# The 256-column low products of a unit, set one by one between the 512-column high products of the next unit

## The chip, the cores and the metric

One core of a Trainium2 chip runs the whole program. The metric is the device time of one execution in microseconds, the median of three runs. Nothing is read from other cores.

## The reference

Two transformer blocks of two layers each work on 256 tokens of width 1024. Around the change only the gated feed-forward layers matter. There are six of them: two in each of the two layers of the first block, and one in each of the two layers of the second. With h the normed and modulated input, each computes

```python
def swiglu(h, w_gu, w_down):
    g, u = jnp.split(h @ w_gu, 2, axis=-1)
    return (jax.nn.silu(g) * u) @ w_down
```

with w_gu of 1024 x 5632 and w_down of 2816 x 1024, in float32. The second block writes the same thing out in line. Between the feed-forward layers stand attention and retention stages, which the change leaves alone.

## The kernel before, in words

**High and low parts.** A float32 matmul is made of products in fp32r. Each operand is split into a high part (the rounded value) and a low part (the rest), and three products are added up in PSUM: high by high, low of the activations by high of the weights, and high of the activations by low of the weights. ScalarE makes the high part of a weight unit (hi_static, L810), VectorE the low part (lo_static, L1355).

**Units and the ring.** Weights come in units of 128 x 1024 float32 (512 KB). SyncE loads them in pairs into a ring of six raw slots; high and low parts have a ring of seven slots each (PARTS). ScalarE may write slot n only when unit n - 7 is used up, which TensorE tells by adding one to mm_done behind the last product of every unit; VectorE takes unit n after hi_done has counted it, and SyncE refills a raw slot after lo_done.

**A feed-forward phase.** The 2816 hidden columns are worked on in 11 strips of 256. Of a strip b, four units hold gate and up weights and two hold the down weights of the strip before. In strips from FIRST_TURNED on (from strip 3 in the first phase, from strip 1 in the five others, 58 strips in all) the weights are the stationary operand: turned_unit (L2363) works on one half strip j (128 hidden columns) and one half q of the contraction. It issues eight *high* products, whose moving operand is 512 columns (high and low part of the 256 tokens side by side, tile hT), with weights_hi stationary (L2368), and then, after waiting for lo_done, eight *low* products of 256 columns (the tokens' high part) with weights_lo stationary (L2373). Units of a strip come in the order (j=0,q=0), (0,1), (1,0), (1,1). The sums of half strip j lie in the two PSUM banks half_banks(j): columns 0 to 255 hold high by high, columns 256 to 511 hold the two cross terms.

**Behind the half strip.** When mm_done has counted the second unit of a half strip, ScalarE copies the cross part (cross, L1004), VectorE adds it (half_sum, L1690), ScalarE applies silu (L1009), VectorE multiplies gate and up (L1695), ScalarE makes the high part of the activation (L1014, ahi) and VectorE the low part (L1703, alo). Between these steps both engines convert weight units in a fixed written order, and VectorE also works off modulation units (mod_unit, L1368), up to six a strip. TensorE may start half strip j of strip b + 1 when half_sum of strip b, half j, is done.

**Down.** After the four turned units of strip b, down (L2377) multiplies the activations of strip b - 1 by its two down units: rows_unit (L2161) issues for each unit eight products of 512 columns with ahi and alo stationary and weights_hi moving (L2169), and after lo_done four with weights_lo moving (L2174), all into banks 0 to 3. In the last strip of a phase only one down unit is done so; last_three (L2178) takes the other three, and waits there for ahi_done and alo_done of the last strip.

The order of the work on every engine is written out by hand; nothing is planned by a program. The statements at the core:

```python
for kind in (1, 0):
    for k in range(4):
        T.matmul(half_banks(j)[:, kind, :], whi[...], hx[:, :, 4 * q + k, :], ...)
pe.wait_ge(S("lo_done"), n + 1)
for kind in (1, 0):
    for k in range(4):
        ins = T.matmul(half_banks(j)[:, kind, 256:512], wlo[...], hhi[:, 4 * q + k, :], ...)
ins.then_inc(S("mm_done"), 1)
```

Of the kernel before, what the change touches and what calls it, by code (L numbers as in the profile page):

```python
# [261 lines left out]
def build(nc, A, out):  # L262
    with ExitStack() as ctx:
# [1867 lines left out]
        def _(pe):  # L2131
# [29 lines left out]
            def rows_unit(slot, ready, c, first, last, hi_, lo_, first_bank=0, act=None):  # L2161

                pe.wait_ge(S("hi_done"), ready)
                for i, src in enumerate((hi_, lo_)):
                    if act is not None:
                        pe.wait_ge(S(("ahi_done", "alo_done")[i]), act)
                    for t in range(NT):
                        for h in range(2):
                            T.matmul(bank[first_bank + 2 * t + h][:, :], src[:, c, P * t:P * (t + 1)], whi[:, slot, 512 * h:512 * (h + 1)],  # L2169
                                     start=first and i == 0, stop=False)  # L2170
                pe.wait_ge(S("lo_done"), ready)
# [161 lines left out]
            for kind, n0, a in phases:  # L2333
# [19 lines left out]
                if kind == "ffn":  # L2353
# [9 lines left out]
                    def turned_unit(n, j, q):  # L2363

                        pe.wait_ge(S("hi_done"), n + 1)
                        for kind in (1, 0):
                            for k in range(4):
                                T.matmul(half_banks(j)[:, kind, :], whi[:, n % PARTS, 256 * k + P * kind:256 * k + P * (kind + 1)], hx[:, :, 4 * q + k, :],  # L2368
                                         start=q == 0 and k == 0, stop=False)
                        pe.wait_ge(S("lo_done"), n + 1)  # L2370
                        for kind in (1, 0):
                            for k in range(4):
                                ins = T.matmul(half_banks(j)[:, kind, 256:512], wlo[:, n % PARTS, 256 * k + P * kind:256 * k + P * (kind + 1)], hhi[:, 4 * q + k, :],  # L2373
                                               start=False, stop=q == 1 and k == 3)
                        ins.then_inc(S("mm_done"), 1)

                    def down(c, j, u0=0, u1=2):  # L2377
                        if FIRST_TURNED[f] == 1 and j == 0:
                            pe.wait_ge(S("alo_done"), STRIPS * f + 1)
                        for u in range(u0, u1):  # L2380
                            rows_unit((c + u) % PARTS, c + u + 1, u, j == 0 and u == 0, False, ahi[:, j % 2], alo[:, j % 2], act=STRIPS * f + j + 1)
# [27 lines left out]
                    for b in range(FIRST_TURNED[f], STRIPS):  # L2409
                        c = n0 + 4 + 6 * (b - 1)  # L2410
                        for j in range(2):
# [8 lines left out]
                            turned_unit(c + 2 * j, j, 0)  # L2420
# [5 lines left out]
                            turned_unit(c + 2 * j + 1, j, 1)  # L2426
                            if b == 1 and j == 0:
                                turn(0, 0)
                        if b < STRIPS - 1:
                            down(c + 4, b - 1)  # L2430
# [476 lines left out]
```

## Time and profile before

| | |
|---|---|
| Median of 3 runs | 1761.82 us (1761.37 to 1762.06) |
| Span of the profiled execution, first to last instruction | 1759.8 us |
| Its own time as a run | not listed; the span is 2.0 us under the median of the runs |
| TensorE (PE) busy | 1732.4 us, 98% of the span |
| TensorE weight loads (PEld) busy | 1470.0 us, 84% |
| VectorE (DVE) busy | 1419.2 us, 81% |
| ScalarE (ACT) busy | 1006.7 us, 57% |
| Granted TensorE clock, mean | 0.999 of full |
| Chain that ended last | TensorE 94%, of it L2368 24% and L2373 12% |

The profile is one execution. "Busy" of TensorE is the union of its matmul records; since matmuls are pipelined, a record is longer than the distance to the next one's start (a 512-column product has a record of 389 ns, and the next starts 227 ns after it). What a product costs the engine is therefore read from the distances between starts, or from the chain of waits, whose pieces are laid end to end.

### The profile page before, as it was taken

The page shows a single profiled execution, that of the slowest core. Times are in us where ns is not written, and L with a number is a line of the kernel's source. Part 1 is how long each engine was busy: PE and PEld are TensorE (multiplying, and loading weights), DVE is VectorE, ACT ScalarE, POOL GpSimd, SP SyncE. Part 2 cuts the span into 40 slices and gives each one's busy share as a digit, 9 for nine tenths or more (in the row PEclk, how much of TensorE's full clock was granted, in tenths as well). Part 3 has the DMA queues.
Part 4 walks back from the last instruction along what each step waited for, and adds up shares of the span by engine and source line. Part 5 has one row for each costly group of instructions (what it writes and reads, how often), then busy time and mean ns, then how long its engine had stood idle before and what let it go on. Part 6 is the DMA issues. An engine that isn't in the chain of part 4 may idle for free.

```text
span 1759.8 us, 24720 instructions
## 1 busy us (share of the span) xinstructions
PE 1732.4 (98%) x9178; PEld 1470.0 (84%) x9178; DVE 1419.2 (81%) x2185; ACT 1006.7 (57%) x1666; POOL 184.0 (10%) x382
## 2 busy tenths in 40 slices
PE   6999999999999999999999999999999999999998
PEld 3888888888888888988888888888888888888886
DVE  7899987898899888878888866579888876688565
ACT  5445577755475556877545644556455544465454
POOL 3021012111111111021110000001110000010000
PEclk9999999999999999999999999999999999999999
DMA  9999742699869985418898654459886483466551
GB/s 352 356 360 393 273 147 83 259 332 337 315 225 340 332 314 205 168 51 317 329 334 291 224 206 158 161 191 333 324 325 249 169 301 146 185 229 245 204 194 70
DMA packets 125144, 441.10 MB, mean 251 GB/s; under 512 B 15248, under 2 KB 18272, under 8 KB 124896
## 3 DMA queue, kind: packets, MB, share of 16 engines
q1 hardware_dynamic: 91024, 316.17, 49.1%
q0 software_dynamic: 33296, 120.12, 18.2%
q10 hardware_dynamic: 704, 3.23, 0.5%
q8 instruction: 73, 1.20, 0.3%
q14 instruction: 47, 0.39, 0.1%
HBM read 438.38 MB, written 1.09 MB: 250 GB/s over the span
## 4 chain that ended last, share of the span: by engine, by line
PE 94%; DVE 2%; DMA 2%; ACT 1%; issue 1%; SPq 0%; DVEq 0%; ACTq 0%
PE banks L2368 24%; PE banks L2169 15%; PE banks L2373 12%; PE banks L2147 11%; PE banks L2174 7%; PE banks L2152 6%; PE banks L2317 2%; PE banks L2321 2%; PE banks L2326 2%; PE banks L2137 1%; PE banks L2139 1%; PE banks L2138 1%; DMA weights_raw<-in_w_mod_first 1%; PE banks L2281 1%; DVE weights_lo L1355 1%
## 5 line engine op out<-in xcount | busy, mean ns | idle before, releaser
L1355 DVE TENSOR_TENSOR weights_lo<-weights_raw,weights_hi 128x1024 fp32r<-128x1024 f32 (+2 forms) x584 | 685.9, 1200 | 67.5 <-ACT weights_hi L810 66.7
L810 ACT ACTIVATE weights_hi<-weights_raw 128x1024 fp32r<-128x1024 f32 (+2 forms) x584 | 584.8, 1036 | 68.3 <-PE banks L2174 21.9
L2368 PE MATMUL banks<-hT,weights_hi 128*128 128x512 f32 x1856 | 464.1, 392 | 0.0
L2368 PEld LDWEIGHTS banks<-hT,weights_hi 128*128 128x128 f32 x1856 | 337.3, 189 | 63.0
L2373 PEld LDWEIGHTS banks<-hT,weights_lo 128*128 128x128 f32 x1856 | 253.2, 190 | 18.1
L1368 DVE CUSTOM_DVE_ANT_0 arena<-arena,mod_acc,vectors 128x1024 f32<-128x1024 f32 x216 | 267.6, 1280 | 0.0
L2373 PE MATMUL banks<-hT,weights_lo 128*128 128x256 f32 x1856 | 258.8, 282 | 0.0
L1004 ACT ACTIVATE arena<-banks 128x512 f32<-128x512 f32 x116 | 69.3, 598 | 323.1 <-PE banks L2373 322.9
L2147 PE MATMUL banks<-weights_hi,hT 128*128 128x512 f32 (+2 forms) x896 | 218.2, 385 | 0.0
L2147 PEld LDWEIGHTS banks<-weights_hi,hT 128*128 128x128 f32 x896 | 165.6, 188 | 29.9
L1690 DVE TENSOR_TENSOR arena<-banks,arena 128x512 f32<-128x512 f32 x116 | 79.8, 688 | 108.9 <-ACT arena L1004 108.9
L2169 PE MATMUL banks<-weights_hi,actT_hi 128*128 128x512 f32 x520 | 140.9, 392 | 0.3 <-DVE window_bias L1405 0.3
L2169 PE MATMUL banks<-weights_hi,actT_lo 128*128 128x512 f32 x520 | 139.3, 390 | 0.0
L2174 PE MATMUL banks<-weights_lo,actT_hi 128*128 128x512 f32 x520 | 139.0, 389 | 0.0
L2152 PE MATMUL banks<-weights_lo,hT 128*128 128x512 f32 (+2 forms) x448 | 116.9, 383 | 0.0
L2169 PEld LDWEIGHTS banks<-weights_hi,actT_lo 128*128 128x128 f32 x520 | 97.6, 188 | 21.1
L2174 PEld LDWEIGHTS banks<-weights_lo,actT_hi 128*128 128x128 f32 x520 | 97.6, 188 | 20.3
L2169 PEld LDWEIGHTS banks<-weights_hi,actT_hi 128*128 128x128 f32 x520 | 93.6, 189 | 16.8 <-DVE window_bias L1405 0.7
L531 POOL DMA_DIRECT2D arena<-in_w_mod x128 | 67.5, 530 | 364.8 <-DVE mod_cols L1368 361.2
L2152 PEld LDWEIGHTS banks<-weights_lo,hT 128*128 128x128 f32 x448 | 83.8, 188 | 15.1
L1009 ACT ACTIVATE arena<-arena 128x256 f32<-128x256 f32 x116 | 48.0, 414 | 74.1 <-DVE arena L1690 74.0
L792 POOL TENSOR_TENSOR x<-x,arena 128x512 f32<-128x512 f32 x10 | 12.7, 1275 | 677.1 <-DVE arena L1513 677.1
(358 smaller groups left out, 1971.3 us busy)
## 6 DMA issues: line engine op xcount, KB each, us to landing
weights_raw<-in_w_ffn_gu SPq DMA_DIRECT2D x176, 512.0 KB, 4.5
arena<-in_w_mod POOLq DMA_DIRECT2D x128, 512.0 KB, 6.2
weights_raw<-in_w_in SPq DMA_DIRECT2D x104, 512.0 KB, 4.1
weights_raw<-in_w_ffn_down SPq DMA_DIRECT2D x88, 512.0 KB, 5.0
arena<-in_w_ada POOLq DMA_DIRECT2D x88, 512.0 KB, 5.6
weights_raw<-in_w_ffn_in SPq DMA_DIRECT2D x88, 512.0 KB, 4.1
weights_raw<-in_w_ffn_out SPq DMA_DIRECT2D x44, 512.0 KB, 4.5
weights_raw<-in_w_out SPq DMA_DIRECT2D x32, 512.0 KB, 3.8
```

The lines of the kernel that those rows point to most:

```text
L531: eng.dma_start(mod_tile(m), mod_rows(m)).then_inc(S(mod_sem(m)), 16)
L810: nc.scalar.activation(whi[:, n % PARTS, 0:width], raw[:, slot, 0:width], ACT.Copy).then_inc(S("hi_done"), credit(n))
L1004: nc.scalar.activation(cross_t[:, j], half_banks(j)[:, :, 256:512], ACT.Copy).then_inc(S("half_by_act"), 1)
L1355: V.tensor_tensor(wlo[:, n % PARTS, 0:width], raw[:, n % RING, 0:width], whi[:, n % PARTS, 0:width].bitcast(F32), ALU.subtract).then_inc(S ...
L1368: V.tensor_tensor_reduce(modw[m % MOD_RING], modw[m % MOD_RING], cond_row, 1.0, vec[:, m:m + 1], ALU.mult, ALU.add, modc[:, m:m + 1])\
L1690: V.tensor_tensor(sum_t[:, j], half_banks(j)[:, :, 0:256], cross_t[:, j], ALU.add).then_inc(S("half_by_dve"), 1)
L2147: T.matmul(bank[banks[t]][:, 0:width], src[:, 2 * u + k, P * t:P * (t + 1)], whi[:, slot, k * width:(k + 1) * width], start=u == 0 and k = ...
L2152: ins = T.matmul(bank[banks[t]][:, 0:width], hi_[:, 2 * u + k, P * t:P * (t + 1)], wlo[:, slot, k * width:(k + 1) * width], start=False, s ...
L2169: T.matmul(bank[first_bank + 2 * t + h][:, :], src[:, c, P * t:P * (t + 1)], whi[:, slot, 512 * h:512 * (h + 1)], start=first and i == 0, ...
L2174: ins = T.matmul(bank[first_bank + 2 * t + h][:, :], hi_[:, c, P * t:P * (t + 1)], wlo[:, slot, 512 * h:512 * (h + 1)], start=False, stop= ...
L2368: T.matmul(half_banks(j)[:, kind, :], whi[:, n % PARTS, 256 * k + P * kind:256 * k + P * (kind + 1)], hx[:, :, 4 * q + k, :], start=q == 0 ...
L2373: ins = T.matmul(half_banks(j)[:, kind, 256:512], wlo[:, n % PARTS, 256 * k + P * kind:256 * k + P * (kind + 1)], hhi[:, 4 * q + k, :], st ...
```

## The change

Three things are new.

1. turned_unit gets the unit before it (before). If there is one, it waits for that unit's lo_done at its own start, and behind each of its eight high products it issues one low product of the unit before (turned_low). The eighth adds to mm_done for the unit before.
2. The low products of the strip's fourth unit go into the first down unit: rows_unit issues one behind each of its eight products with weights_hi moving.
3. In the last strip of a phase the fourth unit's low products stand in a block behind it (last_low), as before. The first unit of a strip has no low products between its high ones.

The products, their operands, the PSUM regions and the number of instructions on ScalarE, VectorE, GpSimd and SyncE are the same.

```diff
-            def rows_unit(slot, ready, c, first, last, hi_, lo_, first_bank=0, act=None):
+            def rows_unit(slot, ready, c, first, last, hi_, lo_, first_bank=0, act=None, low=None, turned_low=None):
...
                             T.matmul(bank[first_bank + 2 * t + h][:, :], src[:, c, P * t:P * (t + 1)], whi[:, slot, 512 * h:512 * (h + 1)],
                                      start=first and i == 0, stop=False)
+                            if low is not None:
+                                turned_low(low, 4 * i + 2 * t + h)
...
-                    def turned_unit(n, j, q):
+                    def turned_low(unit, i):
+
+                        n, j, q = unit
+                        kind, k = 1 - i // 4, i % 4
+                        ins = T.matmul(half_banks(j)[:, kind, 256:512], wlo[:, n % PARTS, 256 * k + P * kind:256 * k + P * (kind + 1)], hhi[:, 4 * q + k, :],
+                                       start=False, stop=q == 1 and k == 3)
+                        if i == 7:
+                            ins.then_inc(S("mm_done"), 1)
+
+                    def turned_unit(n, j, q, before):
 
                         pe.wait_ge(S("hi_done"), n + 1)
...
+                        if before is not None:
+                            pe.wait_ge(S("lo_done"), before[0] + 1)
+                        for i in range(8):
+                            kind, k = 1 - i // 4, i % 4
+                            T.matmul(half_banks(j)[:, kind, :], whi[:, n % PARTS, 256 * k + P * kind:256 * k + P * (kind + 1)], hx[:, :, 4 * q + k, :],
+                                     start=q == 0 and k == 0, stop=False)
+                            if before is not None:
+                                turned_low(before, i)
+
+                    def last_low(unit):
+
+                        pe.wait_ge(S("lo_done"), unit[0] + 1)
+                        for i in range(8):
+                            turned_low(unit, i)
+
+                    def down(c, j, u0=0, u1=2, low=None):
                         if FIRST_TURNED[f] == 1 and j == 0:
                             pe.wait_ge(S("alo_done"), STRIPS * f + 1)
+                        if low is not None:
+                            pe.wait_ge(S("lo_done"), low[0] + 1)
                         for u in range(u0, u1):
-                            rows_unit((c + u) % PARTS, c + u + 1, u, j == 0 and u == 0, False, ahi[:, j % 2], alo[:, j % 2], act=STRIPS * f + j + 1)
+                            rows_unit((c + u) % PARTS, c + u + 1, u, j == 0 and u == 0, False, ahi[:, j % 2], alo[:, j % 2], act=STRIPS * f + j + 1,
+                                      low=low if u == 0 else None, turned_low=turned_low)
...
-                            turned_unit(c + 2 * j, j, 0)
+                            turned_unit(c + 2 * j, j, 0, (c + 1, 0, 1) if j == 1 else None)
...
-                            turned_unit(c + 2 * j + 1, j, 1)
+                            turned_unit(c + 2 * j + 1, j, 1, (c + 2 * j, j, 0))
+                            if b == STRIPS - 1 and j == 1:
+                                last_low((c + 3, 1, 1))
...
-                            down(c + 4, b - 1)
+                            down(c + 4, b - 1, low=(c + 3, 1, 1))
```

## Rows read from the trace of the kernel before

**Rows 1.** The page, part 1: busy us, share of the span, instructions of each engine.

```profile
PE 1732.4 (98%) x9178; PEld 1470.0 (84%) x9178; DVE 1419.2 (81%) x2185; ACT 1006.7 (57%) x1666; POOL 184.0 (10%) x382
```

**Rows 2.** The page, part 5: groups of the two kinds of product, and ScalarE's wait.

```profile
L2368 PE MATMUL banks<-hT,weights_hi 128*128 128x512 f32 x1856 | 464.1, 392 | 0.0
...
L2373 PE MATMUL banks<-hT,weights_lo 128*128 128x256 f32 x1856 | 258.8, 282 | 0.0
L1004 ACT ACTIVATE arena<-banks 128x512 f32<-128x512 f32 x116 | 69.3, 598 | 323.1 <-PE banks L2373 322.9
```

**Rows 3.** Chain of waits, 592 to 625 us, one strip: start us, us, what.

```profile
592.39 1.81 PE banks L2368 x8
594.20 0.95 PE banks L2373 x8
595.16 1.84 PE banks L2368 x8
597.00 0.95 PE banks L2373 x8
597.95 1.84 PE banks L2368 x8
...
602.58 0.95 PE banks L2373 x8
603.54 1.84 PE banks L2169 x8
605.38 0.91 PE banks L2174 x4
```

**Rows 4.** Chain of waits, 240 to 258 us: products of other widths.

```profile
247.44 1.29 PE banks L2147 x8
248.73 0.54 PE banks L2152 x4
...
250.87 0.17 PE banks L2137
251.04 0.17 PE banks L2138
...
253.78 0.76 PE banks L2152 x4
```

**Rows 5.** Timeline of TensorE, same place: widths of those products (start us, us).

```profile
248.57 0.70 PE L2152 MATMUL banks<-weights_lo,actT_hi 128*128 128x288 f32 x4
...
250.71 0.33 PE L2137 MATMUL banks<-weights_hi,actT_hi 128*128 128x384 f32 x1
...
253.61 0.92 PE L2152 MATMUL banks<-weights_lo,hT 128*128 128x416 f32 x4
```

**Rows 6.** Timeline of TensorE, 610 to 613.6 us, in windows that begin ever later.

```profile
610.65 1.11 PE L2373 MATMUL banks<-hT,weights_lo 128*128 128x256 f32 x8
611.61 0.63 PE L2368 MATMUL banks<-hT,weights_hi 128*128 128x512 f32 x2
...
610.77 1.00 PE L2373 MATMUL banks<-hT,weights_lo 128*128 128x256 f32 x7
...
611.84 1.77 PE L2368 MATMUL banks<-hT,weights_hi 128*128 128x512 f32 x7
...
612.08 1.53 PE L2368 MATMUL banks<-hT,weights_hi 128*128 128x512 f32 x6
```

**Rows 7.** Busy time in two strips: us, PE, PEld, DVE, ACT, POOL, clock, DMA.

```profile
114.61:131.23 16.62, 16.62 (x90) 14.34 (x88) 16.62 (x25) 8.46 (x12) 3.75 (x8) 1.00 0.96 361
608.84:625.45 16.61, 16.61 (x89) 14.34 (x88) 14.41 (x21) 8.45 (x13) 2.11 (x4) 1.00 0.90 329
```

**Rows 8.** Timeline, 126 to 137 us: half_sum and TensorE's next use of its banks.

```profile
131.13 0.69 DVE L1690 TENSOR_TENSOR arena<-banks,arena 128x512 f32<-128x512 f32 x1
...
136.79 0.40 PE L2368 MATMUL banks<-hT,weights_hi 128*128 128x512 f32 x1
```

**Rows 9.** Timeline, 495 to 506 us: last strip of the second feed-forward phase.

```profile
495.65 2.00 PE L2368 MATMUL banks<-hT,weights_hi 128*128 128x512 f32 x8
...
495.85 0.60 ACT L1004 ACTIVATE arena<-banks 128x512 f32<-128x512 f32 x1 [5.16 <-PE banks L2373]
...
499.38 1.99 ACT L810 ACTIVATE weights_hi<-weights_raw 128x1024 fp32r<-128x1024 f32 x2
...
501.44 0.60 ACT L1004 ACTIVATE arena<-banks 128x512 f32<-128x512 f32 x1
...
503.71 0.42 ACT L1014 ACTIVATE actT_hi<-arena 128x256 fp32r<-128x256 f32 x1 [0.49 <-DVE arena L1695]
...
505.35 0.39 PE L2196 MATMUL banks<-weights_hi,actT_hi 128*128 128x512 f32 x1
```

More of the change, by code:

```diff
@@ L2361, in _ @@
                     rows_made = made_by_rows(f)
-                    def turned_unit(n, j, q):
-                        pe.wait_ge(S("hi_done"), n + 1)
[L2366 to L2375, printed above, removed]
@@ L2377, in down @@
-                    def down(c, j, u0=0, u1=2):
+                    def turned_low(unit, i):
[5 more added lines that the diff above has]
+                            ins.then_inc(S("mm_done"), 1)
```

## Prediction

> **What bounds the kernel now.** I read the shares first: TensorE is busy 98% of the span [rows 1]. Then the costliest groups: the 1856 high products and the 1856 low products of the turned strips, neither with idle time before it [rows 2]. In the 58 turned strips TensorE never waits, so only the distance from one product to the next can give time, or a new wait can take some. The chain of waits shows these distances without the pipeline's overlap [rows 3]. The reader should see three sizes there. Eight high products behind products of 512 columns take 1.81 us, 226.7 ns each. Eight high products behind a low block take 1.84 us, whether they are turned or down products. Eight low products take 0.95 us, 119 ns each. The granted clock is full in these strips [rows 7].
>
> **What a product costs.** Can the order matter at all? The other widths answer [rows 4, 5]. Four products of 288 columns take 0.54 us (about 133 ns each), one of 384 columns 0.17 us once the stretch has settled, one of 512 columns 226.7 ns, one of 256 columns inside a block about 120 ns. From 256 to 288, 384 and 512 columns the cost grows by about 0.417 ns a column, which is the full clock of 2.4 GHz, and what is left over is the same everywhere: 226.7 - 213.3 = 13.3 ns, and 120 - 106.7 = 13.3 ns. One width is off: 416 columns take 190 ns, 3 more than this line gives. So a low product in its block is not held up by something the wide ones hide; it pays the same fixed 13.3 ns (an estimate, read from these widths). A high and a low product side by side then cost 226.7 + 120.0 = 346.7 ns in any order.
>
> What order can change is the rest. From the second low of a block (610.77) to the first high (611.61) seven lows take 0.84 us, 120 ns each [rows 6]. The whole block takes 0.953 us, so its first low is followed after 113 ns. The highs behind it take 1.841 us instead of 1.813: the first three start at 611.61, 611.84 and 612.08 [rows 6], 0.47 us for two distances that would be 0.453. Low block and highs behind it cost 2.794 us, 349.2 ns for a high and a low, and the 2.5 ns over 346.7 are a tax that the first five or so highs pay. (Check on a strip: 24 x 0.2267 + 4 x 2.794 = 16.62 us; it takes 16.61 [rows 7].)
>
> **The change, part by part.** *Moved:* 58 strips have 4 low blocks each, 232. Six of them (the last unit of each phase) stay in a block with a down unit behind them, and cost what they did. The other 226 are taken apart and go among the 226 blocks of eight highs behind them, 174 turned ones and 52 of the down units. Before: 226 x (0.953 + 1.841) = 631.4 us. After: 1808 pairs at p ns each.
>
> *The bounds of p*, which no row shows, since nowhere before do 512 and 256 columns alternate. From below: the first low product behind a high one is followed after 113.3 ns (as above), and the high before it costs 226.7. If each low behaved as the first of a block and each high as behind a high, p = 340.0, the sum 614.7 us, 16.7 us less. From above: lows at 120 and each high with the mean tax of the highs behind a block, 27.6 / 5 = 5.5 ns (1.841 - 1.813 = 0.028 us over the five that pay it), p = 352.2, the sum 636.8, 5.4 us more. In between lie the fixed cost alone, p = 346.7 (626.8, 4.6 us less), and the same tax per low product as now, p = 349.2 (no change). I take 348.0, the middle of the last two: 629.2 us, **2.2 us less**. Nearest to the pair by its mean of 384 columns is the stretch of 384 columns, whose late products take 0.17 us [rows 4], that is 2 x 173.3 = 346.7 a pair; some of its early ones take 0.18, so part of the tax may stay. That the short first distance counts in full I do not believe, because the first high behind a block gives the 6.7 ns back (0.23 in place of 0.227, the two first ones 0.47 in place of 0.453): the two look like one shift of the start.
>
> The Trainium skill ("TensorE: Matmul & The Clock Gate", on weight loading and the back-to-back gap) says that TensorE pulls weight loads ahead of running matmuls, and puts a load of 128 columns at P/1.2, an estimate of 107 ns here; by it a load fits behind either kind of product. It also states a fixed cost of 2.5 ns a product at full clock, which would make a pair 325 ns; the distances of 226.7 and 120 ns in rows 3 disagree, and they decide.
>
> *The waits of TensorE.* Each paired unit now waits for hi_done and for the earlier unit's lo_done at its start. The first is satisfied long before: ScalarE and VectorE are a strip's part ahead, and no idle time stands before L2368 or L2373 [rows 2]. The second is the wait that stood ahead of the low block, now asked for at the same point of the work. A unit that already waits for two semaphores (597.95, the half strip j = 1) takes the same 1.84 us as one that waits for one (595.16) [rows 3], so one wait more is costed at nothing. Its cover is the running product; without it, each would be some tens of ns.
>
> *mm_done comes later.* A unit's last low product now ends behind the next unit's eight pairs: 8 x 0.227 = 1.8 us later. Who waits for it: ScalarE's copy L1004 (it waits 322.9 us in all for L2373, 105 times [rows 2]), behind it in ScalarE's order the next weights' high parts, behind these VectorE's low parts and SyncE's refills. ScalarE has some 8 us idle in a strip of 16.6 [rows 7], so it catches up. The tightest place in mid-phase is the first phase, where VectorE has no idle time at all in a strip [rows 7]: half_sum ends at 131.82 and TensorE wants the banks at 136.79 [rows 8], 5.0 us of room against 1.8. VectorE there is set by its modulation units, not by the copy. Costed at nothing; if the room went, each strip would lose what is missing.
>
> *The ends of the phases.* The copy for j = 0 of the last strip would start at about 497.6 instead of 495.85 [rows 9]. ScalarE then works without a break through two single conversions, silu, the high part and a double conversion that now ends at 501.37 and would end near 502.7. The copy for j = 1, ready since 501.4, goes from 501.44 to about 502.7, and the activation's high part, which ends at 504.13, to 505.4. TensorE asks for it at 505.35 [rows 9]. So the next thing late is ahi_done, by 0.05 to 0.3 us, in five phases (in the first, VectorE's modulation units set the chain already): **0.7 us more** in all, between 0 and 1.5.
>
> Sum against the profiled execution: 1759.8 - 2.2 + 0.7 = 1758.3 us of span; the median of the runs is 2.0 us above the span, so 1761.8 - 1.5 = **1760.3 us**.
>
> **The rivals.** What a measurement of this kernel can tell from no change is about 0.2%, 3.5 us.
>
> *A. The low product is held up in its block by the weight load beside it* and is free between wide ones: p = 340, 1761.8 - 16.7 + 0.7 = 1745.8 us. For it speaks the first distance of each block, 113 ns; against it that 288 and 384 columns, which leave a load more time, have the same 13.3 ns over their columns. Chance 0.12.
>
> *B. Each high behind a low pays the tax.* Now five of eight highs behind a low block pay, in alternation all eight would be just behind a low one. Price 5.5 ns a pair over 346.7, 1808 times: 1761.8 + 5.4 + 0.7 = 1767.9 us, slower. It decides from p = 350.8 on (3.5 us less the 0.7, over 1808 pairs). For it: the first two highs behind a block pay some 16 ns together, more than half of the 28, and products of 416 columns keep 3 ns too many through a whole stretch [rows 4]. Against: if the tax is a backlog of narrow products that wide ones work off, one low leaves an eighth of it. Chance 0.18.
>
> *C. Nothing, to the last ns:* p = 349.2 and the phase ends hidden, 1761.8. It is within the likeliest case.
>
> *D. The delayed mm_done reaches TensorE in every strip.* 1.8 us against 5.0 us of room makes it unlikely; 58 strips x 0.3 us would be 17 us. Chance 0.02.
>
> **How the numbers follow.** Likeliest, 0.68: p between 346.7 and 349.2 with 0 to 1.5 us at the phase ends, 1757.2 to 1763.3 us. A 0.12, B 0.18, D 0.02. Most of the likeliest case lies within 0.2%; its low edge, p at 346.7, does not, and gets 0.15 of the chance. So faster 0.12 + 0.15 = 0.27, slower 0.18 + 0.02 = 0.20, same 0.53. The range takes in the bounds of p at both ends, since nothing in the trace excludes either: 1745 to 1768.5.
>
> **What would show it.** In the chain of waits of the changed kernel a strip's first unit should still be eight highs in 1.81 us; eight pairs behind it 2.77 to 2.79 us (2.72 if A holds, 2.82 if B), and a whole strip 16.57 us against 16.61 now. L1004 should wait for a product under another line, its cross copies in mid-phase 1.8 us later against the strip, without idle time of TensorE. At the phase ends a gap of up to 0.3 us should stand before L2196. The forecast is wrong if single distances behind a low product are longer than 127 ns or behind a high one longer than 232, if TensorE's idle time in the turned strips is no longer nil, or if pairs run at 340.

## The result, and the profile after

The changed kernel takes **1777.18 us** (median of 4 runs, 1776.62 to 1778.14), the kernel before, run beside it, 1761.94 us (4 runs, 1761.37 to 1762.61). The ratio is 1.0086, 95% interval 1.0072 to 1.0100: slower by 15.2 us. The forecast was 1760.3 with a range up to 1768.5; it is wrong in size and in sign. The profiled execution has a span of 1774.8 us (its own time 1776.62) at a granted clock of 0.998.

The page of the changed kernel: the busy time of each engine, and the groups that answer to [rows 1, 2] (busy us, mean ns of one, idle time before them and what ended it).

```profile
PE 1741.5 (98%) x9178; PEld 1466.7 (83%) x9178; DVE 1420.3 (80%) x2185; ACT 1004.6 (57%) x1666; POOL 184.0 (10%) x382
...
L2381 PE MATMUL banks<-hT,weights_hi 128*128 128x512 f32 x1856 | 599.1, 396 | 0.0
L2369 PE MATMUL banks<-hT,weights_lo 128*128 128x256 f32 x1856 | 512.4, 280 | 0.0
...
L1004 ACT ACTIVATE arena<-banks 128x512 f32<-128x512 f32 x116 | 69.3, 598 | 391.2 <-PE banks L2369 391.2
```

The work is the same: VectorE, ScalarE and GpSimd are busy as long as before. Neither kind of turned product has idle time before it, so whatever was lost inside the strips was lost in the distances between products. TensorE's busy time grew by 9.1 us, the span by 15.0: the rest must be idle time. (The groups' busy sums can't be compared with [rows 2], because records of alternating products overlap.)

**The distances.** Chain of waits of the changed kernel, 592 to 615 us (start us, us, what; a piece with no "x" is a single product): this is the strip that answers to [rows 3].

```profile
597.71 2.04 PE banks L2381 x9
...
601.28 0.24 PE banks L2381
601.52 0.12 PE banks L2369
...
602.34 0.24 PE banks L2381
...
610.82 0.94 PE banks L2176 x4
611.76 1.84 PE banks L2169 x8
```

The nine highs at 597.71 run at the old 226.7 ns. From there on three pairs take 1.06 us (601.28 to 602.34), and so again behind it: **353.3 ns a pair**, not 348.0. Behind the pairs the four L2176 take 0.94 instead of 0.91 and the next eight L2169 1.84 instead of 1.81: the tax that used to fall on the highs behind a low block now falls here as well. A strip, from the start of its first high to that of the next strip's, takes 16.79 us instead of 16.61.

**Two rhythms.** Not every pair takes 353.3 ns. Chain of waits of the changed kernel, 344 to 353 us: the first turned strip of the second phase, in which four transposes of 128 columns (L2406) stand between two units.

```profile
345.23 0.23 PE banks L2381
...
346.29 0.23 PE banks L2381
...
346.98 0.44 PE banks L2406 x4
...
347.76 0.23 PE banks L2381
...
351.92 0.23 PE banks L2381
```

Ahead of the transposes three pairs take 1.06 us, 353.3 ns each. Behind them twelve pairs take 4.16 us, 346.7 ns each, with the same widths and the same loads. Of the 52 distances from one strip to the next within a phase, 12 have one or four such short products between two units. Eleven of these are shorter than before, by 0.02 to 0.06 us; the twelfth (at 1643 us) keeps the slow rhythm and is 0.20 us longer. The 40 others are all longer, by 0.18 us. So 353.3 ns is not what the widths and loads must cost. What puts TensorE on one rhythm or the other is not shown.

**Where the 15.0 us of span are.** From the starts of the turned products in both traces, after less before: the opening stretch to the first turned high, -0.31; the 52 distances from one strip to the next within a phase, +7.0; the last strips' highs, 6 x -0.04; the five stretches from a phase's last turned high to the next phase's first, +1.73, +1.71, +1.69, +1.60, +1.66; the end, +0.13. One low product per phase moved behind the last high (the +0.13 at the end, which has nothing else), so the pairs have cost about 7.5 us and the five phase ends about 8.4 - 5 x 0.13 = 7.7 us.

**The phase ends.** What TensorE waits for (in all us, times, longest). L2198 are the first products that need the last strip's activations. Before, no wait stood ahead of L2196, and L2281, the same transposes as L2283 now, waited for L842 once, 0.8 us. The longest wait of L2198, 1.4 us, is at the end of the first phase (at 215 us); the four others are 0.3 us.

```profile
PE banks L2283 <- ACT arena L842: 3.8, 5, 0.8
PE banks L2198 <- ACT actT_hi L1014: 2.8, 5, 1.4
```

Timeline of VectorE at the end of the second feed-forward phase, the changed kernel; it answers to [rows 9]. Start us, us, what, idle time before it and what ended it. Then two rows of TensorE from the same place.

```profile
507.12 0.69 DVE L1690 TENSOR_TENSOR arena<-banks,arena 128x512 f32<-128x512 f32 x1 [0.20 <-ACT arena L1004]
...
509.20 0.42 DVE L1703 TENSOR_TENSOR actT_lo<-arena,actT_hi 128x256 fp32r<-128x256 f32 x1 [0.48 <-ACT actT_hi L1014]
509.54 2.36 DVE L1355 TENSOR_TENSOR weights_lo<-weights_raw,weights_hi 128x1024 fp32r<-128x1024 f32 x2
...
512.01 0.69 DVE L1513 TENSOR_TENSOR arena<-banks,gate_bcast 128x512 f32<-128x512 f32 x1
```

```profile
509.31 0.47 PE L2198 MATMUL banks<-weights_hi,actT_hi 128*128 128x512 f32 x1 [0.34 <-ACT actT_hi L1014]
...
516.70 0.44 PE L2283 MATMUL banks<-con,arena 128*128 128x128 f32 x2 [0.76 <-ACT arena L842]
```

And VectorE at the same place in the kernel before:

```profile
504.16 0.42 DVE L1703 TENSOR_TENSOR actT_lo<-arena,actT_hi 128x256 fp32r<-128x256 f32 x1 [0.48 <-ACT actT_hi L1014]
...
507.01 0.69 DVE L1513 TENSOR_TENSOR arena<-banks,gate_bcast 128x512 f32<-128x512 f32 x1
```

Both show the same queue: behind alo (L1703) stand two conversions, the scale columns (a 0.16 us piece, left out here) and L1513, which opens the residual sum at the boundary; L1513 starts 2.8 us after L1703 in both, and the view records no wait among them. L1513 leads over the norm and ScalarE's L842 to the transposes L2283. So VectorE was already on the path across the boundary before the change, and a delay of its alo comes out whole on the other side. TensorE's 0.34 us ahead of L2198 is only the first sight of it.

### The profile page after: what moved, and what is told of

The parts are those of the page before. It is cut to its first block, busy times and chain, and to the rows that moved or that the text cites. A ratio compares the mean times of both kernels' runs of the same rounds, so it can differ in the third digit from the quotient of the medians.

```text
span 1774.8 us, 24852 instructions
## 1 busy us (share of the span) xinstructions
PE 1741.5 (98%) x9178; PEld 1466.7 (83%) x9178; DVE 1420.3 (80%) x2185; ACT 1004.6 (57%) x1666; POOL 184.0 (10%) x382
## 4 chain that ended last, share of the span: by engine, by line
PE 91%; DVE 4%; ACT 2%; DMA 1%; issue 1%; SPq 0%; ACTq 0%; DVEq 0%
PE banks L2381 23%; PE banks L2169 14%; PE banks L2369 12%; PE banks L2147 11%; PE banks L2176 7%; PE banks L2152 6%; PE banks L2319 2%; PE banks L2323 2%; PE banks L2328 2%; DMA weights_raw<-in_w_mod_first 1%; DVE weights_lo L1355 1%; PE banks L2137 1%; PE banks L2139 1%; PE banks L2138 1%; PE banks L2283 1%
## 5 line engine op out<-in xcount | busy, mean ns | idle before, releaser
L2381 PE MATMUL banks<-hT,weights_hi 128*128 128x512 f32 x1856 | 599.1, 396 | 0.0
L2369 PE MATMUL banks<-hT,weights_lo 128*128 128x256 f32 x1856 | 512.4, 280 | 0.0
L2381 PEld LDWEIGHTS banks<-hT,weights_hi 128*128 128x128 f32 x1856 | 348.7, 188 | 81.8
L2369 PEld LDWEIGHTS banks<-hT,weights_lo 128*128 128x128 f32 x1856 | 347.4, 189 | 2.3
L1690 DVE TENSOR_TENSOR arena<-banks,arena 128x512 f32<-128x512 f32 x116 | 79.9, 689 | 122.3 <-ACT arena L1004 122.3
L2169 PE MATMUL banks<-weights_hi,actT_hi 128*128 128x512 f32 x520 | 160.1, 395 | 0.0
L2169 PE MATMUL banks<-weights_hi,actT_lo 128*128 128x512 f32 x520 | 159.3, 393 | 0.0
L2176 PE MATMUL banks<-weights_lo,actT_hi 128*128 128x512 f32 x520 | 140.8, 392 | 0.0
L2169 PEld LDWEIGHTS banks<-weights_hi,actT_lo 128*128 128x128 f32 x520 | 97.6, 188 | 22.8
L2169 PEld LDWEIGHTS banks<-weights_hi,actT_hi 128*128 128x128 f32 x520 | 97.0, 188 | 22.2
L2176 PEld LDWEIGHTS banks<-weights_lo,actT_hi 128*128 128x128 f32 x520 | 94.0, 188 | 19.4
L531 POOL DMA_DIRECT2D arena<-in_w_ada x88 | 46.5, 531 | 265.8 <-DVE mod_cols L1368 256.2
```

Source lines behind the costliest of these rows:

```text
L531: eng.dma_start(mod_tile(m), mod_rows(m)).then_inc(S(mod_sem(m)), 16)
L1690: V.tensor_tensor(sum_t[:, j], half_banks(j)[:, :, 0:256], cross_t[:, j], ALU.add).then_inc(S("half_by_dve"), 1)
L2176: ins = T.matmul(bank[first_bank + 2 * t + h][:, :], hi_[:, c, P * t:P * (t + 1)], wlo[:, slot, 512 * h:512 * (h + 1)], start=False, stop= ...
```

## The experiments

Three questions: is the slower pair a property of the alternation, where do the phase ends lose their time, and what holds a pair at 353 ns? The diffs are against the changed kernel unless they say otherwise.

**1. The delay without the alternation.** Each unit's low products still come one unit late, but as a block of eight behind the next unit's highs.

```diff
-                            if before is not None:
-                                turned_low(before, i)
+                            if before is not None and i % 8 == 7:
+                                for e in range(i - 7, i + 1):
+                                    turned_low(before, e)
```

(The same in rows_unit.)

> The low products as late as in the changed kernel, but in a block of eight behind the eight high products of the next unit, so the products alternate as seldom as before. Theory of two parts: a high and a low cost 349 ns as before (a block of lows 0.95 us, the highs behind it 1.84), the strips 16.61 us, and the phase ends still cost their 7.8 us or a little more, since mm_done comes as late: 1769.7 us. If the delay of mm_done also costs in the strips, the strips are longer than 16.61. Rival (order alone): 1762.

1770.12 us, ratio 1.0047 (1.0032 to 1.0062). Chain of waits, 596 to 604 us:

```profile
596.39 3.63 PE banks L2383 x16
600.02 0.95 PE banks L2371 x8
600.98 1.84 PE banks L2383 x8
```

Blocks cost what they did before, wherever they stand. Of the 8.3 us over the kernel before, the strips have 0.2; the rest comes with the delay, at the phase ends. So the two losses are separate and add up.

**2. Pairs in the last strip of each phase only.** turned_unit and down get None in the strips before it, and each unit's low block stands behind it (last_low).

```diff
+                            paired = b == STRIPS - 1
-                            turned_unit(c + 2 * j, j, 0, (c + 1, 0, 1) if j == 1 else None)
+                            turned_unit(c + 2 * j, j, 0, (c + 1, 0, 1) if j == 1 and paired else None)
+                            if not paired:
+                                last_low((c + 2 * j, j, 0))
...
-                            down(c + 4, b - 1, low=(c + 3, 1, 1))
+                            down(c + 4, b - 1, low=(c + 3, 1, 1) if paired else None)
```

> The complement: pairs only in the last strip of each phase (144 pairs), blocks elsewhere. Theory of two parts: 144 x 4.1 ns = 0.6 us, plus the phase ends, 7.8 us: 1770.3 us, with waits of about 0.3 to 1.4 us for ahi_done in five phases. Rival (order alone): 1762.5. Rival (mm_done late in every strip): about 1763.5.

1769.22 us, ratio 1.0044 (1.0027 to 1.0061). The 52 strip distances are those of before (-0.0 us in all), the boundaries of phases 2 to 5 are 1.64, 1.68, 1.62 and 1.65 us longer, the first one 0.71. The first phase's delay thus needs an earlier strip's pairs as well. L2283 waits as in the changed kernel, 3.8 us in all; what L2198 waits for:

```profile
PE banks L2198 <- ACT actT_hi L1014: 1.7, 5, 0.3
```

**3. The last strip in blocks, pairs in all others.** As experiment 2, with the opposite condition.

```diff
+                            paired = b < STRIPS - 1
```

> The changed kernel, but in the last strip of each phase the low products stand in blocks behind their units again. Theory: the loss of 15.2 us has two parts that add up, 353.3 instead of 349.2 ns for each alternating pair (1808 pairs, +7.4 us), and the last strip's late mm_done, which makes ScalarE and VectorE late at five phase ends (+7.8 us). Then only 1664 pairs stay, +6.8 us, and no wait before L2198-like lines at the phase ends: 1768.8 us. Rival (all of it is the order of the products, the waits at the ends are there anyway): about 1776. Rival (all of it comes from mm_done being late in every strip): about 1775, since 52 of 58 strips keep that.

1776.88 us, ratio 1.0085 (1.0070 to 1.0100): a miss. The boundaries still lose 1.66, 1.48, 1.60, 1.35 and 1.42 us, though in the last strip ScalarE's copy comes in time. VectorE's sum for j = 0 of that strip was 1.7 us late all the same. Timeline of VectorE, 499 to 504 us, the last of four modulation units in a row and the sum:

```profile
502.22 1.28 DVE L1368 CUSTOM_DVE_ANT_0 arena<-arena,mod_acc,vectors 128x1024 f32<-128x1024 f32 x1
...
503.43 0.69 DVE L1690 TENSOR_TENSOR arena<-banks,arena 128x512 f32<-128x512 f32 x1
```

Ahead of the sum (L1690) stand VectorE's own modulation units, back to back and without idle time, and they were late from the strip before. From the sum of strip 9's j = 0 on, VectorE can give almost nothing back. In the kernel before it idles there 0.3 us, then 0.38 us ahead of the last strip's second sum, and twice 0.48 us behind that, waiting for ScalarE's steps in the same half strip. Only the 0.38 us shrink here, to 0.20, and the delay from 1.7 to 1.5 us.

**4. Also strip 9's last low block put back before its down units.** Strip 10, the last, blocked as in experiment 3; down of strip 9 gets no low products, which stand in a block ahead of it (last_low).

```diff
-                            down(c + 4, b - 1, low=(c + 3, 1, 1))
+                            down(c + 4, b - 1, low=(c + 3, 1, 1) if b < STRIPS - 2 else None)
```

> As the run with the last strip in blocks, and in addition the low products of the last but one strip's fourth unit stand in a block ahead of its down units. Theory: in the earlier run the late mm_done of that fourth unit (it came with the down unit's pairs) made VectorE 1.7 us late, and VectorE, without idle time between there and half_sum of the last strip, carried it into the phase end; with this block in place the phase ends are as before, and 1656 pairs at 4.1 ns remain: 1761.8 + 6.8 = 1768.6 us, no wait of 0.3 us for ahi_done or 0.8 us for the scaled x at the phase ends. Rival (something else of the earlier strips, such as the late copies of j = 0, makes VectorE late): 1775 to 1777 as before.

1775.97 us, ratio 1.0083 (1.0066 to 1.0100): a second miss, boundaries +1.79 to +1.55 us. The copy for j = 1 of strip 9 was repaired; the one for j = 0 of strip 9 was still late, and the delay reached the boundary. Experiment 5 tells whether that copy is enough.

**5. The last two strips in blocks.** As experiments 2 and 3, with this condition.

```diff
+                            paired = b < STRIPS - 2
```

> Pairs in all strips but the last two of each phase, which are as before. Theory, formed on the trace of the run before it: from half_sum of strip 9, half j = 0, to the end of the phase VectorE has no idle time, so a copy L1004 that is 1.8 us late anywhere in the last two strips is carried to the phase end; ahead of that VectorE idles some 2 us and takes the delay up. Then the phase ends are as in the kernel before, and 1472 pairs at 4.1 ns remain: 1761.8 + 6.0 = 1767.8 us. If the delay comes from still earlier strips: about 1775.

1769.67 us, ratio 1.0043 (1.0026 to 1.0059). Now the boundaries are back: +0.57, +0.02, +0.11, -0.07, -0.04 us. TensorE's waits:

```profile
PE banks L2283 <- ACT arena L842: 0.8, 1, 0.8
...
PE banks L2198 <- ACT actT_hi L1014: 0.4, 1, 0.4
```

From experiment 4 this differs only in the low products of strip 9's first three units, and the delay is gone. In phases 2 to 5 the sums of strip 8 are still 1.7 us late and those of strip 9 are not. VectorE idles ahead of strip 9's first sum (2.1 us in experiment 3's trace) and takes the delay up there. In the first phase the last sums stay 0.6 us late, which is its boundary's 0.57. The strips cost 5.9 us more, which with the 0.6 makes 6.5; the median is 7.9 above. In the profiled execution the opening stretch, which the edit does not touch, was 1.83 us longer; the other profiled executions have it between -0.8 and +1.8 against before. The 1.4 us stay unassigned.

**6. Pairs only inside a half strip.** The second unit of each half carries the first one's low products; its own stand in a block behind it. So the half's last mm_done, for which the copy waits, is no later than before.

```diff
-                            turned_unit(c + 2 * j, j, 0, (c + 1, 0, 1) if j == 1 else None)
+                            turned_unit(c + 2 * j, j, 0, None)
...
-                            if b == STRIPS - 1 and j == 1:
-                                last_low((c + 3, 1, 1))
+                            last_low((c + 2 * j + 1, j, 1))
...
-                            down(c + 4, b - 1, low=(c + 3, 1, 1))
+                            down(c + 4, b - 1)
```

> One by one only inside a half strip: the second unit's high products take the first unit's lows between them, the second unit's lows follow in a block. The products alternate in half of the places, and the second mm_done of a half strip, for which the copy waits, comes when it did. Theory: nothing late at the phase ends; per half strip 8 pairs at 353.3 ns in place of a low block and taxed highs (2.794 us), 0.032 us, 116 times, 3.7 us: 1765.5 us. Rival (half of the whole loss, order alone): 1769.

1764.30 us (10 runs), ratio 1.0014 (1.0005 to 1.0023). Boundaries +0.03, +0.11, +0.27, +0.03, +0.12 us, no wait ahead of the ahi products, 1.9 us in the strips. With 928 pairs of 1808 left, the strips lose 1.9 us, where 3.7 were expected, and the loss at the ends is gone with the late signal.

**7, 8. Groups of two and of four.** As in experiment 1 with 2 or 4 in place of 8.

```diff
+                            if before is not None and i % 2 == 1:
+                                for e in range(i - 1, i + 1):
+                                    turned_low(before, e)
```

> Two high, two low products in turn (in place of one and one). Read from the distances in the strips, over 13.3 ns a product: one low between highs costs 6.7 ns at its return, eight or sixteen lows 20 ns at theirs. If a backlog grows with each low and is full after three, two lows cost 13.3 ns: 353.3 ns a pair as with one. If it is full after two: 20 / 2, 356.7 ns a pair. If only the first pair of the alternation matters: 350.0. Total near 1777 or, with 20 ns, 1783.

> Four high, four low products in turn. With a full backlog of 20 ns at each return: 346.7 + 5.0 = 351.7 ns a pair, total about 1774 (+4.5 us for the order, +7.8 at the phase ends). If the tax is 2.5 ns a low product as in blocks of eight: 349.2, total 1770.

1769.41 us with two, 1773.18 us with four (one run each). Chains of waits, with two and with four:

```profile
599.97 0.47 PE banks L2383 x2
...
601.37 0.47 PE banks L2383 x2
```

```profile
600.21 0.93 PE banks L2383 x4
...
603.02 0.93 PE banks L2383 x4
```

Two at a time take 1.40 us for four pairs here (599.97 to 601.37), and 1.39 in the neighbouring stretches, 348.5 ns a pair; a strip takes 16.59 us, 0.03 less than before. Four at a time take 2.81 us for eight (600.21 to 603.02), 351 ns, strips of 16.69. All three theories for two put them at 350 ns a pair or more: a miss. Four came as expected. The cost does not simply fall with the group's length. Less the low products that moved behind the last high, the boundaries lost 1.5 to 1.8 us each in both.

**9. Half a strip in blocks.** From the kernel before: both units' highs, then both units' lows.

```diff
-                            turned_unit(c + 2 * j, j, 0)
+                            turned_highs(c + 2 * j, j, 0)
...
-                            turned_unit(c + 2 * j + 1, j, 1)
+                            turned_highs(c + 2 * j + 1, j, 1)
+                            turned_lows(c + 2 * j, j, 0)
+                            turned_lows(c + 2 * j + 1, j, 1)
```

> The kernel before, with the two units of a half strip taken together: 16 high products, then 16 low ones. The copy behind a half strip starts when it did. Theory that the tax is paid at each return from low to high products, some 20 ns over 13.3 ns a product, whatever the length of the low block: two such returns a strip instead of four, 58 x 2 x 0.020 = 2.3 us less than before, 1759.6 us. Rival (the tax is proportional to the number of low products): no change, 1761.9. Rival (the first unit's slot, freed 2.8 us later, holds up ScalarE): slower, with waits in the strips.

1759.71 us (10 runs, against 13 of before), ratio 0.9989 (0.9980 to 0.9999). Chain of waits, one strip:

```profile
592.05 3.63 PE banks L2368 x16
595.68 1.91 PE banks L2376 x16
597.59 3.65 PE banks L2368 x16
...
603.16 1.84 PE banks L2169 x8
```

This is the fastest version of this study that computes the same as the reference, as expected at 1759.6. It is 2.1 us under the kernel before; the interval just excludes no difference, and the gain is smaller than the 0.2% that the forecast took as the least one can tell. A return from low to high products costs some 20 to 30 ns whether 8 or 16 lows came before (3.65 against 3.63, 1.84 against 1.81). The strip has two returns instead of four and takes 16.57 us. The half's last signal is not later, and the boundaries keep their length.

**10 to 12. Other widths of the low product,** one by one between the highs as in the change. (In the first, the lows cover half of their tokens only; in the other two the sums are not those of the reference's formula.)

```diff
-                        ins = T.matmul(half_banks(j)[:, kind, 256:512], ..., hhi[:, 4 * q + k, :],
+                        ins = T.matmul(half_banks(j)[:, kind, 256:384], ..., hhi[:, 4 * q + k, 0:P],
```

(For 384 and 512 columns: `[:, kind, 0:384]` with `hx[:, :, 4 * q + k, 0:192]`, and `[:, kind, 0:512]` with `hx[:, :, 4 * q + k, :]`.)

> One by one as in the changed kernel, but the low products take only the first 128 tokens (the low part of the weights is left out for the other 128), so they are 128 columns wide instead of 256. Theory of a fixed 13.3 ns a product plus 6.7 ns a pair: 640 / 2.4 + 26.7 + 6.7 = 300 ns a pair. Rival (a weight load beside a narrow product sets its pace): the transposes of 128 columns never follow each other faster than 108 ns in the kernel before, so a pair costs 227 + 108 to 120 = 335 to 347 ns. Nothing is claimed for the total.

> One by one, low products 384 columns wide (the low part of the weights then multiplies other columns than it should, so the cross terms are wrong by what that part gives). With 13.3 ns a product and no tax: 400.0 ns a pair; with 6.7 ns a pair: 406.7. The pair with 128 columns took 340.0 (no tax, but the narrow product was held at 113 ns), the one with 256 columns 353.3.

> One by one, low products 512 columns wide (they multiply the tokens' low part too, a term that is otherwise left out). All products are then equally wide and still alternate between two weight tiles and two PSUM regions. If the tax comes of narrow products among wide ones: 453.3 ns a pair, no tax. If it comes of the alternation of tiles or banks: 460 or more.

1757.29, 1871.96 and 1955.81 us (one run each). Chains of waits at 128, then 384 columns:

```profile
600.09 0.28 PE banks L2381
600.37 0.06 PE banks L2369
600.43 0.28 PE banks L2381
```

```profile
640.14 0.23 PE banks L2381
640.37 0.17 PE banks L2369
```

A pair with a low of 128 columns takes 340.0 ns (the rows repeat every 0.34 us), with 384 in most strips 406.7, with 512 453.3. Half the low's columns save only 13.3 ns: from the start of a high to the start of the low behind it pass 280 ns instead of 227. This was the rival's result, a load that sets the pace; a product of fixed cost plus columns would have given some 300. Experiment 15 tests it.

**13 to 15. Half the load.** The turned products with 64 stationary columns instead of 128: the kernel before so, the changed one so, and the changed one so with lows of 128 columns. Half of the gate and up columns are left out in all three. The high products of the down units keep 128 stationary columns.

```diff
-T.matmul(half_banks(j)[:, kind, :], whi[:, n % PARTS, 256 * k + P * kind:256 * k + P * (kind + 1)], hx[:, :, 4 * q + k, :],
+T.matmul(half_banks(j)[0:64, kind, :], whi[:, n % PARTS, 256 * k + P * kind:256 * k + P * kind + 64], hx[:, :, 4 * q + k, :],
```

(The same for the low products.)

> The kernel before, but the turned units load 64 instead of 128 stationary columns for every product (half of the gate and up columns are left out). If the 13.3 ns over the columns, or the 120 ns of a low product in its block, come from the length of the weight load, blocks of lows go faster, to 113 or 107 ns each, and highs under 227. If the 13.3 ns are a fixed cost of a product: 120 and 226.7 as before.

> The changed kernel with 64 stationary columns a product in the turned units (half of the gate and up columns are left out). If the 6.7 ns a pair come from the weight load that runs beside the narrow product: 346.7 ns a pair in the turned units, or 340, and 353 still in the down units' pairs, whose high products keep 128 stationary columns. If they come from the mixed widths of the moving operand: 353.3 as before.

> As the run with 128-column low products (340.0 ns a pair), with 64 stationary columns a product in the turned units (half of the gate and up columns and the low part for half of the tokens are left out). If the narrow product was held at 113 ns by the load beside it, the pair falls to the 293 to 300 ns of the columns and the fixed cost. If 113 ns is a floor of a product that does not depend on the load: 340 again.

1757.46, 1760.05 and 1710.59 us (one run each, before beside them 1761.23). Chains of waits. Blocks (13):

```profile
600.33 1.84 PE banks L2368 x8
602.17 0.92 PE banks L2373 x8
```

Pairs (14), first with a turned high, then with one of a down unit (L2169):

```profile
600.22 0.23 PE banks L2381
...
600.56 0.23 PE banks L2381
...
603.28 0.23 PE banks L2169
603.51 0.11 PE banks L2369
603.62 0.23 PE banks L2169
```

Pairs with a low of 128 columns (15), in the same order:

```profile
596.18 0.23 PE banks L2381
...
596.47 0.23 PE banks L2381
...
603.20 0.28 PE banks L2169
603.48 0.06 PE banks L2369
603.54 0.28 PE banks L2169
```

*Low of 128 columns.* With half loads throughout, a pair falls from 340.0 to 291 ns. In the down units, where only the high's load is whole, it stays at 340. Timeline of experiment 15, weight load and product:

```profile
603.66 0.19 PEld L2169 LDWEIGHTS banks<-weights_hi,actT_hi 128*128 128x128 f32 x1
...
603.66 0.22 PE L2369 MATMUL banks<-hT,weights_lo 128*64 128x128 f32 x1
```

So the load of the next high product starts together with the low one, and it is this load, beside the narrow product, that sets the pace there.

*Low of 256 columns.* In pairs the 13.3 ns vanish: 340.0 ns. They vanish in the down units too, where the load beside the low product is still whole and only the low's own load, which runs beside the wide product, is halved; the expectation had 353 there, a miss. So the 13.3 ns are not explained by the load beside the narrow product alone. In a block the low products settle at 113.3 ns instead of 120 (eight take 0.92 us), but the high ones get no faster, as was expected, but slower: eight turned ones take 1.84 us in every unit, 230 ns each. Eight and eight in blocks are then 2.76 us, 345 ns for a high and a low: with half loads alternation is the cheaper order.

## Why the prediction was wrong

**"A low product in its block is not held up by something the wide ones hide; it pays the same fixed 13.3 ns": this step failed.** It was read from a line through four widths. Once its loads are halved a low product takes 113.3 ns (experiments 13 and 14), so 6.7 of the 13.3 ns over its 106.7 were no fixed cost. 512 and 256 columns then both take 0.443 ns a column, with nothing left over. For the widths between, the line is neither confirmed nor refuted: 288, 384 and 416 columns took 133, 173 and 190 ns, 3 to 6 ns above 0.443 a column, with whole loads only. The 190 ns, where the line gave 187, were noted in the prediction and passed over.

**The pair at 348.0 ns: mis-sized.** In 41 of the 52 strip distances it settles at 353.3, beyond even the bound of 352.2. The 1808 pairs and what their tax puts on the products behind them cost 7.5 us more than the blocks, where the sum had 2.2 less. The bound was worked out from a mean tax of the highs behind a block; alternation was not what that row shows. Some stretches do run at 346.7, a settled high plus a settled low. That they do is not shown to come of a fixed cost, which did not stand; but it shows that with the same widths and loads a pair can also cost less than in blocks.

**Rival A** had p = 340. No settled stretch of pairs with whole loads comes down to it; with half loads it is what comes (experiment 14). So the load does hold up the low product in its block, as the rival said, but setting it between wide ones does not free it. **Rival B** gave a tax per pair, 5.5 ns over 346.7; with 352.2 its size is nearly what came in most strips, and the sign too. Its total, 1767.9, is short by 9.3 us, of which 7.0 are the phase ends and the rest the strips. Its mechanism, a tax on each high behind a low, is not told apart by the chain: the period is 1.06 us for three pairs, and the extra ns fall now on one product, now on the other. As a fixed tax it is ruled out by the stretches at 346.7.

The Trainium skill ("TensorE: Matmul & The Clock Gate", section "LDWEIGHTS (loading the stationary operand)") puts the load of 128 columns at P/1.2, an estimate of 107 ns, by which it would fit beside a low product of 113.3 ns with 6 ns to spare. In experiment 10, where the load sets the pace, the pair stays at 340.0, 113.3 ns over a high one's 226.7. If that is the load's time, an estimate from these two, the measured value decides and leaves no room beside 256 columns.

**The waits of TensorE inside the strips, at nothing: right.** No idle time stands before either kind of turned product, and delayed blocks (experiment 1) run in strips of 16.61 us.

**mm_done 1.8 us later, at nothing in mid-phase: right.** Experiment 1 again: 0.2 us over 52 strips. Rival D falls with it.

**The ends of the phases, 0.7 us: this step failed,** by a factor of eleven, 7.7 us. The first link was right: TensorE waits for ahi_done, 0.34 us at four of the five boundaries (0.05 to 0.3 were forecast). The step stopped there. ScalarE and TensorE were followed, but VectorE's queue behind alo was not: two conversions and L1513 without a break, which decide when the next norm and the transposes begin. Nor did I ask whether VectorE could catch up before: from strip 9's first sum on it has hardly any idle time that it could give back, and so a late sum there reaches the boundary almost whole, 1.5 to 1.7 us. Experiments 2, 3, 4 and 5 show it: pairs in the last strip alone are enough to delay four boundaries. Putting blocks back in the last strip, or also behind strip 9's fourth unit, does not mend them; putting them back in both strips does. Experiment 6, which has pairs in all strips but no later signal for the copy, has no such loss. The first phase, which I held to be set by its modulation units, lost as much as the others (+1.73), and there TensorE's wait for ahi_done was the longest, 1.4 us.

## What to carry to other kernels

When each product loads its own stationary operand, a narrow product can be held up by a load wherever it stands. Before interleaving narrow products with wide ones, halve the load in one run and see whether the narrow product gets faster. A mean distance can also hide two rhythms: look at several stretches, above all behind an odd product, before calling one number the cost. Fewer returns from narrow to wide (sixteen and sixteen instead of eight and eight) gave 0.1% here; single alternation cost 0.4%. When a change makes a signal later, follow it past the first engine that waits: the in-order queue of every engine behind it, up to the next point where all engines meet, and ask at which place that engine last has idle time.

## What the runs showed of the hardware

The cost of a high and a low product in settled alternation, in ns, by the low one's width and the size of the loads. The last column is 0.443 ns a column, summed over both products.

| low columns | both loads 128 columns | high 128, low 64 | both loads 64 | columns alone |
|---|---|---|---|---|
| 128 | 340.0 | 340 to 342 | 291 | 283.3 |
| 256 | 353.3 or 346.7 | 340.0 | 340.0 | 340.0 |
| 384 | 406.7 or 413.3 | not run | not run | 396.7 |
| 512 | 453.3 | not run | not run | 453.3 |

With a low of 128 columns the high's whole load, which runs beside the low product, sets the pace. At 256 and 384 columns up to 13.3 and 16.7 ns are left over with whole loads, and at equal widths nothing. At 256 they go when the low's own load is halved, though that load runs beside the wide product; so the load has a part in it, and how it acts stays open. The two values at 256 columns are the two rhythms: in strips with a short product between two units the pairs mostly take 346.7. At 384 columns it is the other way round: in some of the strips with such a product they take 413.3 instead of 406.7.

By the length of the groups, with 256 columns and in strips without such short products: 353.3 ns a pair alone, 348.5 by twos, 351 by fours, 349.2 by eights, 348.0 by sixteens. That it does not simply fall was not expected, and no run here says why.
